# Shared expert moved from the route into the expert loop of a two-layer mixture-of-experts backbone

## The reference

```
x = x + g2 * moe_ffn(modulate(rms_norm(x, norm2_g), sh2, sc2))

def moe_ffn(h, router_w, router_bias, w_gate, w_up, w_down, ws_gate, ws_up, ws_down):
    affinity = sigmoid(h @ router_w)                      # 64 experts
    idx = top_k(affinity + router_bias, 6)
    gates = affinity[idx] / sum(affinity[idx]) * 2.5
    y = sum over the six experts e of gate * swiglu(h, w_gate[e], w_up[e], w_down[e])
    return y + swiglu(h, ws_gate, ws_up, ws_down)         # the shared expert
```

## Time and profile before

| | us |
|---|---|
| three runs | 2946.36, 2951.84, 2951.17 (median 2951.17) |
| profiled execution | 2948.95, its span 2947.2 |
| prepare, mixer0 | 0 to 235, to 762 |
| layer 0: route, loop's prologue, loop, combine | 762.9, 887.7, 918, 1698.9 to 1747.6 |
| s5_mixer | to 2155 |
| layer 1: route, loop's prologue, loop, combine | 2155.7, 2244.3, 2272.2, 2910.6 to 2947.2 |
| TensorE busy, its weight loads | 2262.6 (77%), 1306.1 |
| VectorE, ScalarE, GpSimd busy | 965.4, 602.9, 569.8 |
| DMA | 684 MB, mean 232 GB/s |

### The profile page before, as it was taken

How to read it: one execution, slowest core, us unless ns; L and a number is a source line. 1 busy time by engine, 2 the same in 40 slices (tenths; PEclk the granted TensorE clock), 3 DMA queues, 4 the chain that set the end, 5 groups by cost and what they waited for, 6 DMA issues and landing times. The chain is left out here.

```text
span 2947.2 us, 41851 instructions
## 1 busy us (share of the span) xinstructions
PE 2262.6 (77%) x12118; PEld 1306.1 (44%) x12119; DVE 965.4 (33%) x2075; ACT 602.9 (20%) x1018; POOL 569.8 (19%) x470
## 2 busy tenths in 40 slices
PE   3995997669596999999999406339966999988881
PEld 2893543444343444444444206337433444444441
DVE  4742237662322111211111146861232111111113
ACT  2232224330211121212212004021021211211110
POOL 2540000000102222222222130400001222222322
PEclk9998999879797999999999757557987999999996
DMA  9983100100509999999999274314035999999994
GB/s 321 353 292 129 57 29 0 72 1 0 211 36 357 347 363 349 367 353 355 357 354 327 77 241 156 80 48 170 0 154 229 378 357 353 364 335 392 391 382 145
DMA packets 177204, 684.02 MB, mean 232 GB/s; under 512 B 34298, under 2 KB 36794, under 8 KB 132346
## 3 DMA queue, kind: packets, MB, share of 16 engines
q1 hardware_dynamic: 129642, 581.86, 51.3%
q0 software_dynamic: 38848, 71.14, 10.1%
q10 hardware_dynamic: 8624, 29.82, 2.5%
HBM read 628.15 MB, written 94.65 MB: 245 GB/s over the span
## 5 line engine op out<-in xcount | busy, mean ns | idle before, releaser
L1369 PE MATMUL pGUw_m<-wguw_m,xTw_m 128*128 128x512 f32 x800 | 358.6, 601 | 21.8 <-issue 21.8
L1380 PE MATMUL pGUn_m<-wgun_m,xTn_m 128*64 128x256 f32 x2816 | 323.3, 382 | 27.9 <-issue 27.9
L1380 PEld LDWEIGHTS pGUn_m<-wgun_m,xTn_m 128*64 128x64 f32 x2816 | 210.9, 137 | 171.7 <-issue 98.2
L1369 PEld LDWEIGHTS pGUw_m<-wguw_m,xTw_m 128*128 128x128 f32 x800 | 149.1, 191 | 232.7 <-issue 232.7
L1419 PE MATMUL pYn_m<-wdn_m,hidTn_m 128*64 128x512 f32 x704 | 189.9, 615 | 19.0 <-DVE hidTn_m L1324 16.6
L1398 PE MATMUL pYw_m<-wdw_m,hidTw_m 128*128 128x512 f32 x400 | 191.8, 602 | 15.5 <-DVE hidTw_m L1310 15.5
L1173 POOL DMA_INDIRECT xgw_m<-moe_h,idxw_m x58 | 60.4, 1042 | 652.1 <-PE pTw_m L1355 619.7
L819 POOL MEMSET zero_r<- 128x1024 f32 x2 | 1.9, 951 | 793.2 <-POOLq L69 523.7
L1179 POOL DMA_INDIRECT xgn_m<-moe_h,idxn_m x96 | 101.1, 1054 | 249.9 <-DVE idxn_m L1300 212.0
L1200 POOL DMA_INDIRECT moe_acc<-yn_m,idxn_m x88 | 140.5, 1597 | 27.5 <-issue 27.5
L1307 DVE TENSOR_TENSOR hidw_m<-hsilw_m,pGUw_m 128x256 f32<-128x256 f32 x50 | 21.1, 421 | 329.2 <-ACT hsilw_m L1242 329.2
(11 more groups left out here) (378 smaller groups left out, 3498.8 us busy)
## 6 DMA issues: line engine op xcount, KB each, us to landing
wgun_m<-in_exp_w_gate SPq DMA_DIRECT2D x88, 1024.0 KB
wgun_m<-in_exp_w_up SPq DMA_DIRECT2D x88, 1024.0 KB
wdn_m<-in_exp_w_down SPq DMA_DIRECT2D x88, 1024.0 KB
wguw_m<-in_exp_w_gate SPq DMA_DIRECT2D x50, 1024.0 KB
wguw_m<-in_exp_w_up SPq DMA_DIRECT2D x50, 1024.0 KB
wdw_m<-in_exp_w_down SPq DMA_DIRECT2D x50, 1024.0 KB
w_p<-in_mod_w SPq DMA_DIRECT2D x24, 2048.0 KB
acc_c<-moe_acc SPq DMA_DIRECT2D x30, 512.0 KB, 10.8
```

The costliest lines, as they stand in the source:

```text
L1369: last = pe.matmul(pGU_w[:], xT_w[b % 2][:, k, :], wgu[0][b % WIDE_RING][:, :, k, :], start=(k == 0), stop=(k == KD - 1))
L1380: last = pe.matmul(pGU_n[H * side:H * side + H, b % 2], xT_n[b % 2][:, k % 4, H * (k // 4):H * (k // 4) + H], w[:, :, k, P * side:P * side ...
```

## The change

- `prepare`: the K products of four groups go to four bands of output partitions (at 32g), ordered so that neighbours differ in their band; four copies and a cleared `KT` go with it.
- `mixer0`: clears all accumulators of both layers (15 MB) behind its last weight load; each layer has its own, and the shared output a buffer of its own.
- `moe_route`: no clears, no shared expert, no wait for its weights ahead of TensorE's first work; a tile's logits follow the next tile's transposes; ranks follow the mask; the table goes through eight small products on TensorE (`pTab`) and a copy.
- `moe_loop`: tile 0 of the shared expert runs in the prologue, its eight products one behind each pick; tile q + 1 runs in group q at b = 3, as `shared_head` (transposes, gate and up) and `shared_tail` (hidden transposes, down), with a step `wide_stored` between them under the wide condition. SP reloads the rows from device memory. The narrow weight ring and the wide gather buffers go from three to two, `y_w` from two to one, and the narrow gate/up's output has one buffer. A group as a whole stands under one more condition.
- `moe_combine`: four parts; TensorE adds three of them with identity products, VectorE the fourth; loads of tile t wait for the sum of tile t − 2.

```diff
--- before.py
+++ after.py
...
             sp.dma_start(w_out, io['ar_w_out'][0].rearrange("(k p) n -> p k n", p=P)).then_inc(wout_in, 16)
+            sp.wait_ge(zero_done, 1)
+            for acc in st['accs']:
+                sp.dma_start(acc.rearrange("(t p) d -> p t d", p=P),
+                             zero[:].rearrange("p (o d) -> p o d", o=1).to_broadcast([P, acc.shape[0] // P, D])).then_inc(acc_zero, 16)
+            sp.wait_ge(acc_zero, 16 * len(st['accs']))
...
-WIDE_RING, NARROW_RING = 2, 3
+WIDE_RING, NARROW_RING = 2, 2
+SHARED_AT = 3
...
-            sp.wait_ge(tab_done, 1)
-            sp.dma_start(tab_dram, tabi[:]).then_inc(tab_out, 16)
-            sp.wait_ge(tab_out, 16)
-            sp.dma_start(table[:], tab_dram[0:ROWS, :].rearrange("(o a) b -> o (a b)", o=1)).then_inc(tab_in, 16)
-            for t in range(NT):
-                sp.wait_ge(y_done, t + 1)
-                sp.dma_start(accs[0][t * P:(t + 1) * P, :], ysh[:, t % 2, :]).then_inc(y_out[t % 2], 16)
             sp.wait_ge(h_out, 16 * NT)
-            sp.wait_ge(tab_in, 16)
-            for b in range(2):
-                sp.wait_ge(y_out[b], 16 * (NT // 2))
-            sp.wait_ge(zero_out, 16 * 2 * NT)
+            sp.wait_ge(wsload, 48)
...
-            act.wait_ge(zero_done, 1)
-            for acc in accs[1:]:
-                for t in range(NT):
-                    act.dma_start(acc[t * P:(t + 1) * P, :], zero[:]).then_inc(zero_out, 16)
...
-            pe.wait_ge(wload, 80)
-            for t in range(NT):
+
+            def rows(t):
...
-            gate_up(0)
-            for t in range(NT):
-                if t + 1 < NT:
-                    gate_up(t + 1)
-                down(t)
-                if t == 1:
-                    ranks()
...
+            rows(0)
+            pe.wait_ge(wload, 32)
+            for t in range(1, NT):
+                rows(t)
+                logits(t - 1)
+            logits(NT - 1)
+
+            pe.wait_ge(mask_done, 1)
+            pe.wait_ge(aff_done, 1)
+            for t in range(NT + 1):
+                col = pL[:, t * NE:(t + 1) * NE]
+                for u in range(min(t + 1, NT)):
+                    last = pe.matmul(col, (upper if u == t else ones)[:], maskb[:, u, :],
+                                     start=(u == 0), stop=(u == min(t + 1, NT) - 1))
+            last.then_inc(rank_mm, 1)
+
+            pe.wait_ge(tab_done, 1)
+            for c in range(8):
+                last = pe.matmul(pTab[:, c, 0:ROWS], tabf[:, c:c + 1], ident[:, 0:ROWS], start=True, stop=True)
+            last.then_inc(tab_mm, 1)
...
         def trips(eng, n_wide, n_narrow, steps):
 
+            n_both = eng.value_load(table[0:1, 3:4], min_val=(NT - 1) * UNROLL, max_val=max(most_wide, NE))
             with eng.Fori(0, TRIPS) as q:
-                for b in range(UNROLL):
-                    i = q * UNROLL + b
-                    for kind, step in steps:
-                        with eng.If((n_narrow if kind else n_wide) > i):
-                            step(i, q, b)
+                with eng.If(n_both > q * UNROLL):
+                    for b in range(UNROLL):
+                        i = q * UNROLL + b
+                        for kind, step in steps:
+                            if kind < 2:
+                                with eng.If((n_narrow if kind else n_wide) > i):
+                                    step(i, q, b)
+                            elif b == kind - 2:
+                                with eng.If(q < NT - 1):
+                                    step(q)
...
+            def shared_rows(q):
+                sp.wait_ge(Z['y_out'], q * 16 + 16)
+                first = nc.s_assert_within((q + 1) * P, P, (NT - 1) * P,
+                                           skip_runtime_bounds_check_because="the step stands under q < NT - 1")
+                sp.dma_start(xy_s[:], h_dram[bass.ds(first, P), :]).then_inc(Z['rows_in'], 16)
+
+            sp.dma_start(xy_s[:], h_dram[0:P, :]).then_inc(Z['rows_in'], 16)
...
+            def shared_rows(t):
+                pe.wait_ge(Z['rows_in'], t * 16 + 16)
+                rows = xy_s[:].rearrange("p (a c k) -> p a k c", a=2, k=KD // 2)
+                for half in range(2):
+                    if half:
+                        pe.wait_ge(Z['xT_done'], t * 2 + 1)
+                    for k in range(4):
+                        last = pe.transpose(pT_w[:, k * P:(k + 1) * P], rows[:, half, k, :], ident[:])
+                    last.then_inc(Z['xT_mm'], 1)
+                pe.wait_ge(Z['xT_done'], t * 2 + 2)
+
+            def shared_up(k):
+                return pe.matmul(pGU_w[:], xT_s[:, k, :], wsgu[:, :, k, :], start=(k == 0), stop=(k == KD - 1))
+
+            def shared_down(t):
+                pe.wait_ge(Z['hid_done'], t + 1)
+                for k in range(2):
+                    last = pe.transpose(pHT[:, k, :], hid_w[:].rearrange("p (c k) -> p k c", k=2)[:, k, :], ident[:])
+                last.then_inc(Z['hidT_mm'], 1)
+                pe.wait_ge(Z['hidT_done'], t + 1)
+                for half in range(2):
+                    for k in range(2):
+                        last = pe.matmul(pY_w[:, half * 512:(half + 1) * 512], hidT_w[:, k, :],
+                                         wsd[:, k, half * 512:(half + 1) * 512], start=(k == 0), stop=(k == 1))
+                last.then_inc(Z['y_mm'], 1)
+
+            def shared_head(q):
+                shared_rows(q + 1)
+                for k in range(KD):
+                    last = shared_up(k)
+                last.then_inc(Z['gu_mm'], 1)
+
+            def wide_stored(i, q, b):
+                if b == SHARED_AT:
+                    pe.wait_ge(W['y_done'], i + 2)
+
+            def shared_tail(q):
+                shared_down(q + 1)
+
+            def shared_stored(q):
+                pe.wait_ge(Z['y_done'], q + 2)
+
+            shared_rows(0)
             for i in range(AHEAD):
                 for kind in range(2):
+                    if i:
+                        pe.wait_ge(S[kind]['idx_done'], i)
                     pick(kind, i)
-                    pe.wait_ge(S[kind]['idx_done'], i + 1)
+                    last = shared_up(2 * i + kind)
+            last.then_inc(Z['gu_mm'], 1)
+            for kind in range(2):
+                pe.wait_ge(S[kind]['idx_done'], AHEAD)
+            shared_down(0)
...
+            pe.wait_ge(Z['y_done'], 1)
+            trips(pe, n_wide, n_narrow,
+                  ((0, up_wide), (1, up_narrow), shared_at(SHARED_AT + 1, shared_stored), (0, rest_wide), (1, rest_narrow),
+                   shared_at(SHARED_AT, shared_head), (0, wide_stored), shared_at(SHARED_AT, shared_tail)))
...
-        @block.gpsimd
-        def _(pool):
+        @block.tensor
+        def _(pe):
             for t in range(NT):
-                pool.wait_ge(acc_in[t], 48)
-                pool.tensor_tensor(acc1[:, t, :], acc1[:, t, :], acc2[:, t, :], ALU.add).then_inc(half_sum, 1)
+                pe.wait_ge(acc_in[t], 64)
+                if t >= 2:
+                    pe.wait_ge(summed, t - 1)
+                for half in range(2):
+                    c = slice(half * 512, (half + 1) * 512)
+                    for k in range(1, 4):
+                        last = pe.matmul(pS[t % 2][:, c], ident[:], slot(k, t)[:, c], start=(k == 1), stop=(k == 3))
+                last.then_inc(part_sum, 1)
...
-                    act.activation(KT[half][:], pK[0:SI, :].rearrange("p (g c) -> p g c", g=4)[:, :, 0:15 * SI],
-                                   ACT.Copy).then_inc(S['kt_done'], 1)
+                    if at == 0:
+                        act.wait_ge(S['kt_zero'], 2)
+                    for g in range(4):
+                        act.activation(KT[half][32 * g:32 * g + SI, :], pK[32 * g:32 * g + SI, 0:15 * SI], ACT.Copy).then_inc(S['kt_done'], 1)
...
-                    for g in range(4):
-                        gg = n * GB + 4 * half + g
-                        for d, k0, c0 in ((1, 1, 0), (0, 0, 7 * SI)):
-                            for part in range(2):
-                                last = pe.matmul(pK[0:SI, g * 256 + c0:g * 256 + c0 + SL * SI], Bd[d][:, part, gg, :],
+                    for d, k0, c0 in ((1, 1, 0), (0, 0, 7 * SI)):
+                        for part in range(2):
+                            for g in range(4):
+                                last = pe.matmul(pK[32 * g:32 * g + SI, c0:c0 + SL * SI], Bd[d][:, part, n * GB + 4 * half + g, :],
```

More of the change, by code:

```diff
@@ L945, in _ @@
                                           op0=ALU.mult, op1=ALU.mult))
-            done.wait()
-            for part in range(3):
-                done(dve.tensor_copy(pick_rhs[:, :, :, 2 + part], gate[:]))
-                done.wait()
-                if part < 2:
-                    done(dve.tensor_tensor(gate[:], gate[:], pick_rhs[:, :, :, 2 + part], ALU.subtract))
-                    done.wait()
-            shared_hidden(1)
-            shared_hidden(2)
```

(31 more changed lines are left out.)

271 lines of the change are left out of this document (135 added, 136 removed).

## The result

The changed kernel takes 3042.8 us (median of four runs, 3041.6 to 3048.8) against 2951.5 before: a ratio of 1.031, with a 95% interval of 1.029 to 1.034. It is 91 us slower where 19 were forecast, and lies outside the range. Its profiled execution took 3041.6 us, span 3039.9, which is 92.7 above the span of before.

The account below looks back on a forecast made before the run. The prediction took TensorE and its sequencer, not transfers, to set the expert loops' pace. Its terms, −26 − 111 + 20 + 136 + 22 + 6 − 42 + 16, gave +21, 2970 us; range 2925 to 3000.

Parts of the forecast that it names:

- What bounds the loop: Both expert loops: TensorE and its sequencer set the pace, not transfers, so work added to TensorE's program adds time.
- Buffers: Expert loops: two narrow weight slots for three, one wide gather pair and one y_w less, cost 0.
- The fetch rule: Trainium skill: taken branches outside fetched pages wait for a DMA fetch; the jump over a group might cost more, unsized.
- Shared tile: Expert loops: a shared tile takes 17.0 us with nothing else running, +136 for eight; bounds 101 and 152.
- Rival A: Shared tile cheaper in the loop, 12.7 us for 17.0, if copies and silu hide: −34, 2936 us; chance 0.20.
- Prologue: Loop prologues: shared tile 0 adds 10 us in each layer, +20; bounds 8 and 30.
- Extra condition: Expert loops: the wide_stored condition on TensorE, 0.25 us in each of 88 items, +22; bounds 0 and 26.
- Combine: Combine: transfers also bring the shared part, +9 and +7; TensorE's sums even; +16, bounds 0 and 47.
- rival D: Combine and prologue at half clock reach their high bounds: +30, 3000 us; chance 0.07.
- Routes: Both layers' routes: clears gone, logits and ranks sooner, shorter chain to the loop: −111; bounds −100 and −118.
- ends: Empty ends of the loops: fewer false conditions to pass, −31 and −11, −42 in all; bounds −30 and −48.
- prepare: Prepare: K products in four bands save TensorE 40 us, then transfers end the stretch: −26; bounds 0 and −31.

Follow-up runs that it names:

- a_merge: The changed kernel with 40 filler memsets, step wide_stored removed, its wait moved to the end of rest_wide, shared head and tail under one condition: 3003.3 us.
- a_loads: The changed kernel with 40 filler memsets, combine's first part given a buffer for every tile and all its loads issued at once: 2978.6 us.

## Why the prediction was wrong

- **What bounds the loop: right.** The shared tiles add their whole time, and the transfers' share fell to 0.89 in layer 0's loop.
- **Buffers: wrong, but not the cause of the result.** The third narrow slot was forecast at 0 and is worth 16 us in the kernel before. In the changed kernel, whose narrow items take 9 us and more, its loss does not show; in a_merge, at 8.7 us an item, it does.
- **The step that failed: the loop's code was taken as free of its position.** The sum had no term for instruction fetch inside the loop. The fetch rule was cited and looked for in the one long jump of the group condition, where it costs nothing, and not in the loop's own jump back. It is worth 45 us in layer 1's expert block: with nothing but VectorE's code shifted, the change stands at 2992 us, 22 above the forecast and inside its range. That it comes so near is in part luck, since the shared tiles cost less than forecast and most other terms more.
- **Shared tile: mis-sized.** Forecast 17.0, measured 15.1 in the trace and 14 to 15.5 by removal. The 1.0 for conditions and registers does not show: the next gate/up starts at 945.30, before the down records end. Rival A was right in direction, but a tile stayed above the 14.4 at which it decides by most of these readings, and the other terms ate the gain.
- **Prologue: mis-sized, +26.5 for +20.** From the block's first clear to the first gate/up it takes 13.8 and 12.7 us more than before. This lies within the stated bounds; no run separates its parts.
- **Extra condition: right in sum, wrong in its parts.** Forecast 0.25 in all 88 items; measured 0.31 in narrow-only ones and 0.14 in pairs, so 38 × 0.31 + 50 × 0.14 = 19 us for the forecast 22. The false shared steps, 0.54 in each of the eight groups without a shared tile, and about 0.1 a group for its own condition come to the 6 forecast; this is an estimate from the gaps above.
- **Combine: mis-sized, +28 for +16.** The transfers' traffic was counted, the added wait on SP was not, though the change's text has it. By a_loads, which takes that wait away, it is 13 us by the median and 16 by the two stages. What was left, 9, comes with TensorE's sums, which set the pace there, and hardly with the traffic that the term was made of; rival D, whose price was sums at the lower clock, was there in part (the granted clock is 0.74 and 0.71 in the two combines).
- **Routes −103.5 for −111, ends −36 for −42, prepare −20.5 (−25 alone) for −26: right**, each a few us short. The ends' shortfall is layer 1's: its 25 conditions left were to take 7 us and the end takes 11.3, where layer 0's 28 take 8.2 as forecast. The prediction counted these conditions, so the cause is another and stays open.
- **The sum of the misses** in the stage table: +47 and −7 for the expert blocks, +12, +7.5, +6 and +5.5 for the rest, 71 us of the 72 between the forecast of +21 and +92.7.

## What to carry to other kernels

A hardware loop has a length and a place. When an edit, anywhere ahead, moves a loop's first instruction, look for idle time that ends with "issue" on an engine at the same point of every round, and for more packets on the instruction queues; a few dozen dummy instructions in front tell in one run whether it is the place. A queue with a busy share near 1 does not say that the stage waits for it: find a stretch where it is half empty and compare the period. And work that ran beside other engines' waits should not be moved to a stretch whose pace its own engine sets.

## What the runs showed that I had not expected

- VectorE's loop costs 7 to 8 us more a round of narrow-only items at one place and nothing 18 instructions before or 42 behind it. The changed kernel fetched 42 more packets of 8.1 KB, the kernel before with 18 fillers 50 more.
- A condition not met costs TensorE 0.29 us where nothing else happens and 0.31 us between narrow items; where the condition is met, 0.14 us.
- Behind a pause of 1.96 us in a_merge and behind the stalls of the changed kernel TensorE's granted clock was 0.50: four 512-column records took 1.98 and 1.97 us in place of 1.08. In the item of the stall the lower clock added 0.6 us.
- Prepare's length varied between 210 and 216 us among kernels in which it is the same, and between 235 and 241 among those with the old K products.
